# The second residual projection of an encoder layer walked by token tile instead of by column half, and the preparation of the two FFN products moved around it

## The reference, cut to what matters

```python
    om = jnp.einsum('bhqm,bmhd->bqhd', p, mem_v.astype(jnp.float32)).reshape(bx, t, MEM_WIDTH)
    x = x + om.astype(x.dtype) @ w_mo                      # 512 -> 1024 columns
    h = rmsnorm(x, norm_ffn)
    x = x + jnp.square(jax.nn.relu(h @ w_ffn1)) @ w_ffn2   # 1024 -> 4096 -> 1024
```

## Time and profile before

| | |
|---|---|
| runs | 1749.38, 1750.48, 1750.35 us |
| profiled execution | 1747.89 us, its span 1745.9 us, granted clock 0.99 |
| TensorE matmul busy | 1666.5 us, 95% of the span |
| DVE, ACT, POOL busy | 1178.3, 805.7, 33.8 us |
| projection mo | about 938 to 996 us of the span |
| first FFN product | 995 to 1374 us |
| second FFN product | from 1374.8 us |

### The profile page before, as it was taken

How to read it: one execution, slowest core, us unless ns; L and a number is a source line. 1 busy time by engine, 2 the same in 40 slices (tenths; PEclk the granted TensorE clock), 3 DMA queues, 4 the chain that set the end, 5 groups by cost and what they waited for, 6 DMA issues and landing times. The chain is left out here.

```text
span 1745.9 us, 26833 instructions
## 1 busy us (share of the span) xinstructions
PE 1666.5 (95%) x10590; PEld 1483.1 (85%) x10590; DVE 1178.3 (67%) x1742; ACT 805.7 (46%) x1275; POOL 33.8 (2%) x49
## 2 busy tenths in 40 slices
PE   9999999999999988999999979999999999999998
PEld 8877777889999988888977879999999878787876
DVE  6577877666757599557163785656666867767676
ACT  5577777763434356214173543333323333333344
POOL 1000000000000002001000100000000000000001
PEclk9999999999999999999999999999999999999999
DMA  5232121201011242620280313333334933434322
GB/s 191 76 85 78 49 78 49 78 25 51 27 54 39 59 152 87 251 68 25 73 217 14 133 34 131 139 139 139 139 139 168 351 133 129 149 133 157 121 96 110
DMA packets 157694, 190.50 MB, mean 109 GB/s; under 512 B 5505, under 2 KB 117761, under 8 KB 155522
## 3 DMA queue, kind: packets, MB, share of 16 engines
q1 hardware_dynamic: 157570, 188.79, 32.8%
HBM read 134.58 MB, written 54.20 MB: 108 GB/s over the span
## 5 line engine op out<-in xcount | busy, mean ns | idle before, releaser
L620 PE MATMUL PS<-sbuf_h_hi,sbuf_w_hi 128*128 128x384 f32 x600 | 211.7, 353 | 6.0 <-ACT sbuf_g_N L631 2.7
L622 PE MATMUL PS<-sbuf_h_hi,sbuf_w_lo 128*128 128x384 f32 x600 | 201.7, 336 | 0.0
L621 PE MATMUL PS<-sbuf_h_lo,sbuf_w_hi 128*128 128x384 f32 x600 | 201.5, 336 | 0.0
L2656 PE MATMUL PS<-sbuf_ops_w,sbuf_go_u 128*128 128x512 f32 x448 | 177.1, 395 | 8.6 <-DVE sbuf_gg_X L2746 8.6
L2657 PE MATMUL PS<-sbuf_ops_w,sbuf_go_u 128*128 128x512 f32 x448 | 175.5, 392 | 0.0
L2658 PE MATMUL PS<-sbuf_ops_w,sbuf_go_u 128*128 128x512 f32 x448 | 175.4, 391 | 0.0
L2493 PE MATMUL PS<-sbuf_ops_S,sbuf_ops_w 128*128 128x288 f32 x512 | 152.8, 298 | 11.2 <-ACT sbuf_ff_u L2522 4.6
L2497 PE MATMUL PS<-sbuf_ops_S,sbuf_ops_w 128*128 128x288 f32 x512 | 152.5, 298 | 0.0
L2495 PE MATMUL PS<-sbuf_ops_S,sbuf_ops_w 128*128 128x288 f32 x512 | 152.2, 297 | 0.0
L620 PEld LDWEIGHTS PS<-sbuf_h_hi,sbuf_w_hi 128*128 128x128 f32 x600 | 113.2, 189 | 16.2 <-issue 10.0
L2522 ACT ACTIVATE sbuf_ff_u<-PS 128x576 f32<-128x576 f32 x64 | 41.6, 650 | 177.7 <-DMA uD<-sbuf_ff_sums 97.6
(11 more groups left out here) (317 smaller groups left out, 3919.1 us busy)
## 6 DMA issues: line engine op xcount, KB each, us to landing
sbuf_gg_u<-uD SPq DMA_DIRECT2D x28, 1024.0 KB, 5.1
uD<-sbuf_ff_u SPq DMA_DIRECT2D x16, 1152.0 KB, 4.2
sbuf_ff_raw<-w_ffn SPq DMA_DIRECT2D x16, 1024.0 KB, 6.3
sbuf_gg_B<-w_ffn SPq DMA_DIRECT2D x16, 1024.0 KB, 7.8
sbuf_raw<-w_in SPq DMA_DIRECT2D x28, 512.0 KB, 4.8
uD<-sbuf_ff_sums SPq DMA_DIRECT2D x16, 768.0 KB, 6.3
sbuf_X<-x_prompt SPq DMA_DIRECT2D x16, 512.0 KB, 7.3
xD<-sbuf_X SPq DMA_DIRECT2D x9, 512.0 KB, 2.6
```

What stands on the lines that cost most here:

```text
L620: pe.matmul(out, hi, h_hi[:, kb, tok], start=kb == 0, stop=False)
L621: pe.matmul(out, hi, h_lo[:, kb, tok], start=False, stop=False)
L622: last = pe.matmul(out, lo, h_hi[:, kb, tok], start=False, stop=kb == KB - 1)
L2656: pe.matmul(out, u_hi, x_hi, start=first, stop=False, skip_group_check=True)
```

## The change

The projection's two halves are taken in turn: two tiles of half 0 ahead, then (half 1, tile t) and (half 0, tile t + 2) alternating, by the list `MO_SEQ`. So each tile is complete earlier and its norm starts earlier. ACT's and DVE's lists around it (`mo_act`, `mo_dve`) are new. The sums S1 and S2 are cut in two pieces at token 320 of 576 (`CUT`), and S2's raw form shares S4's rows. At the start of the first FFN product the sums, cuts of weights and evacuations stand in another order. In the second product, `add(k, t)` stands ahead of `blocks` instead of behind, and the sums of the last unit come behind the additions of product k = 1. SP loads `u_unit(1)` ahead of the blocks B12 and B22, and stores the last unit after `u_unit(3)`; the load of weight unit 1 comes behind the projection's tile 6.

```diff
-                    *((row_at(a_rows[x][1]), x, (KH, HT)) for x in ("S1", "S2", "S3", "S4")),
+                    *((row_at(a_rows[x][1]), x, (KH, HT)) for x in ("S1", "S3", "S4")),
+        a_raw["S2"] = a_raw["S4"]
...
+        CUT = 5 * HT // 9
+        MO_SEQ = [(0, 0), (0, 1)] + [x for t in range(NT - 2) for x in ((1, t), (0, t + 2))] + [(1, NT - 2), (1, SMP)]
...
+        def mo_act(act):
+            for t in range(NT):
+                norm_square(act, n_ff, t)
+                if 1 <= t < SMP:
+                    ff_high(act, t - 1)
+                if t == SMP - 2:
+                    w_high(act, 0)
+                    w_high(act, 1)
+            act.wait_ge(N["lo"], 2 * (n_ff.base + SMP - 1))
+            sum_high(act, "S1", 0)
+            w_high(act, 2)
+            ff_high(act, SMP - 1)
+            act.wait_ge(a_sum.sem, a_sum.n(1))
+            sum_high(act, "S2", 0)
+            w_high(act, 3)
...
+            added(0, 0)
+            added(0, 1)
+            f_blocks(dve, 0)
+            for t in range(SMP):
+                added(1, t)
+                if t == SMP - 1:
+                    w_low(dve, 0)
+                norm_mean(dve, n_ff, t)
+                if t == SMP - 1:
+                    w_low(dve, 1)
+                norm_scale(dve, n_ff, t)
+                if 1 <= t < SMP - 1:
+                    ff_low(dve, t - 1)
+                if t + 2 < NT:
+                    added(0, t + 2)
+            added(1, SMP)
+            ff_low(dve, SMP - 2)
+            norm_mean(dve, n_ff, SMP)
+            dve.wait_ge(N["lo"], 2 * (n_ff.base + SMP - 1))
+            sum_raw(dve, "S2", "S1", "A11", 0)
+            norm_scale(dve, n_ff, SMP)
+            sum_low(dve, "S1", 0)
+            w_low(dve, 2)
+            ff_low(dve, SMP - 1)
...
+            left_over(FF_AT["P6", 0])
+            act.wait_ge(a_sum.sem, a_sum.n(3))
+            sum_high(act, "S4")
+            left_over(FF_AT["P7", 0])
+            for k in range(9, 13):
+                w_high(act, k)
...
+            out_of("X11", 0)
+            w_low(dve, 3)
+            ff_low(dve, SMP)
+            dve.wait_ge(N["lo"], 2 * (n_ff.base + NT))
+            sum_raw(dve, "S2", "S1", "A11", 1)
+            w_low(dve, 4)
+            sum_low(dve, "S1", 1)
+            w_low(dve, 5)
+            dve.wait_ge(a_sum.sem, a_sum.n(2))
+            sum_low(dve, "S2", 0)
+            sum_low(dve, "S2", 1)
+            w_low(dve, 6)
+            sum_low(dve, "S3")
+            w_low(dve, 7)
+            dve.wait_ge(a_low.sem, a_low.n(4))
+            sum_raw(dve, "S4", "A12", "S2")
+            w_low(dve, 8)
+            out_of("X11", 1)
+            sum_low(dve, "S4")
+            out_of("X22", 0)
+            f_blocks(dve, 1)
+            for k in range(9, 13):
+                w_low(dve, k)
...
                 if by_tile(k) and kb == 0:
                     for t in tiles_of_product(k):
+                        add(k, t)
                         if t in (0, 1):
                             for h in range(2):
                                 blocks(g, ("T4", "T1")[t], h)
-                        add(k, t)
+                    if k == 1:
+                        token_sums(dve, LASTU)
...
             block_unit("B21", 0)
-            block_unit("B12", 0)
-            sp.wait_ge(f_p, FF_AT["P5", LASTU] + 1)
-            block_unit("B22", 0)
             sp.wait_ge(f_p, FF_AT["P7", LASTU] + 1)
             u_unit(1)
+            block_unit("B12", 0)
+            block_unit("B22", 0)
             u_unit(2)
```

More of the change, by code:

```diff
@@ L1767, in out_pe, with out_act @@
                         norm_turn(pe, norm, t - 2)
-        def out_act(act, round0, nkb, norm, first=lambda act, p: None,
-                    between=lambda t: None, after=None):
+        def out_act(act, round0, nkb, norm, first=lambda act, p: None, between=lambda t: None):
             passes = nkb // 2
@@ L2435, in mo_behind, with part, sum_high, sum_low @@
[L2435 to L2439, removed]
+        def part(x, i):
+            return x[:, :, (0, CUT)[i]:(CUT, HT)[i]]
+        def sum_high(act, x, i=None):
+            hi, raw_ = (a_hi[x], a_raw[x]) if i is None else (part(a_hi[x], i), part(a_raw[x], i))
+            act.activation(hi, raw_, ACT.Copy).then_inc(a_cut.sem, 1)
+        def sum_low(dve, x, i=None):
+            dve.wait_ge(a_cut.sem, a_cut.n(SUM_CUT[x, i]))
+            lo, raw_, hi = (y if i is None else part(y, i) for y in (a_lo[x], a_raw[x], a_hi[x].bitcast(F32)))
+            dve.tensor_tensor(lo, raw_, hi, ALU.subtract).then_inc(a_low.sem, 1)
@@ new lines, in sum_raw, with mo_pe @@
+        def sum_raw(dve, x, y, z, i=None):
+            out, p, m = (a_raw[w] if i is None else part(a_raw[w], i) for w in (x, y, z))
+            dve.tensor_tensor(out, p, m, ALU.subtract).then_inc(a_sum.sem, 1)
+        def mo_pe(pe):
+            y, add = mo_s
+            for n, (p, t) in enumerate(MO_SEQ):
+                if t == 0:
+                    for s in pass_slots(p):
+                        wait_unit(pe, unit(R_MO, s), s)
+                if n >= len(MO):
+                    pe.wait_ge(add, n - len(MO) + 1)
+                mo_ready(pe, p, t)
+                out = PS[:, MO[n % len(MO)], :]
+                tok = slice(t * P, (t + 1) * P)
+                for j in range(4):
+                    s = pass_slots(p)[j // 2]
+                    cols = slice((j % 2) * 512, (j % 2 + 1) * 512)
+                    pe.matmul(out, h_hi[:, j, tok], w_hi[s][:, cols], start=j == 0, stop=False)
+                    pe.matmul(out, h_lo[:, j, tok], w_hi[s][:, cols], start=False, stop=False)
+                    last = pe.matmul(out, h_hi[:, j, tok], w_lo[s][:, cols], start=False, stop=j == 3)
+                    if t == SMP and j % 2:
+                        last.then_inc(slot_free[s], 1)
+                if t < SMP:
+                    last.then_inc(y, 1)
+                if p and 1 <= t < SMP:
+                    if t == 2:
+                        pe.wait_ge(CN["lo"], len(ogroups))
+                    norm_turn(pe, n_ff, t - 1)
@@ L2506, in ff1_act, with left_over @@
         def ff1_act(act):
[L2507 to L2512, removed]
+            def left_over(s):
+                what, n = FF[s]
                 if what in ("P1", "P6", "P7", "P4"):
@@ L2564, in out_of @@
                 dve.wait_ge(x_sq.sem, x_sq.n(n + 1))
[L2565 to L2576, removed]
+                if n < LASTU:
+                    token_sums(dve, n)
@@ L3107, in _ @@
             load_gain(a["norm_ffn"], D)
-            for s in range(2):
-                sp.wait_ge(slot_free[s], unit(R_MO, s)[0] + 2)
-            pair_unit(1)
             for t in range(NT):
-                sp.wait_ge(mo_s[1], NT + t + 1)
+                if t == SMP - 1:
+                    for s in range(2):
+                        sp.wait_ge(slot_free[s], unit(R_MO, s)[0] + 2)
+                    pair_unit(1)
+                sp.wait_ge(mo_s[1], MO_AT[1, t] + 1)
                 sp.dma_start(xD[t], X[:, t, :]).then_inc(xl[t], 16)
```

112 lines of the change are left out of this document (56 added, 56 removed).

## The result

The changed kernel takes 1738.71 us (median of 4 runs, 1738.27 to 1741.96) beside 1750.23 for the kernel before (4 runs): the ratio is 0.9941, 95% interval 0.9929 to 0.9953. That is 11.5 us less, where 19.5 were forecast; 1738.71 lies just above the range. The profiled execution is the slowest of the four, 1741.96 us.

What follows compares the result with a forecast made beforehand. TensorE, busy for 95% of the span, was taken as the bound, so only its waits and clock could be won. 11.6 + 7.0 + 0.9 = 19.5 us off 1750.35 gave 1730.8 us, range 1727 to 1738.5.

Steps and rivals of the forecast that it cites:

- The projection, 0: Projection: same matmuls, additions and transposes in another order; no gain taken for it.
- Start of the first product, 11.6 us: Start of the first FFN product: shorter TensorE waits give 11.6 us, two half-clock stretches of 1.6 and 1.7 included.
- The steps up to P4: First product's start: P1 of unit 1 at 1004.0, P5 1011.0, P6 1014.15, P7 1018.35, P4 1022.95.
- From here on all runs as before: First product, past P6 of unit 1: nothing further changes, so the 11.6 us gained are kept.
- C: Rival, chance 0.14: loads come late, of weight unit 1 (3 us) or in the second product (2 to 5); 1733 to 1740.
- Start of the second product, 7.0 us: Second product before T3's addition: 4.2 us less waiting and 2.8 for the clock, with 0.3 of 4.5 left.
- the other turns, 0.9: Second product at k = 8, 15, 22: the same order takes away 0.43 each; two seen, 0.9 us counted.
- its alternative: Second product's start: loads share evenly, `u_unit(1)` lands at 1381.6 as before; gain 2.3 us, or 5.1 with the clock.
- The sums moved behind k = 1 cost 2.7 there ... covered, by 1 us: Second product: TensorE's two ready pieces last 5.5 us, DVE needs 4.5 to the third, so the moved sums cost nothing.
- the row of the prediction: DVE's 2304-column instructions: 2.55 us long but 2.47 from start to start, so most of the fixed cost is hidden.
- the rule weighed beside it: Cutting S1 and S2: each DVE instruction pays a fixed cost; three more cost about 0.5 us, 19.1 instead of 19.6.
- Rival B: Chance 0.20: clock falls before P1 of unit 1, around P4 (1.6 each) or at k = 1 (up to 2.8); 1732 to 1737.

Runs made afterwards that it cites:

- first_only: The kernel before with the projection's and the first product's edits alone, the second product's undone: 1740.67 us, ratio 0.9959.
- evac_first: The changed kernel with DVE's low cuts of weight pieces 17 and 18 in unit 1 behind the evacuation of P5: 1737.68 us, ratio 0.9931.
- second_only: The kernel before with the second product's edits alone (addition first, last unit's sums behind k = 1, loads ahead of the store): 1746.52 us, ratio 0.9987.
- sums_back: The changed kernel with the last unit's sums and its store back at their old places: 1734.97 us, ratio 0.9916.
- store_later: The changed kernel with only the last unit's store one place later, behind u_unit(4): 1738.77 us, ratio 0.9933.
- evac_first_k2: The changed kernel with evac_first's order, the last unit's sums behind the additions of k = 2 and its store ahead of u_unit(6): 1730.43 us, ratio 0.9890.
- whole_sums: The changed kernel with S1 and S2 summed and cut whole again, behind the last tile: 1741.09 us, ratio 0.9948.
- after_again: The changed kernel measured once more, unaltered, as a base on the same chip: 1740.98 us, ratio 0.9948.
- pool_blocks: The changed kernel with last unit's sums and store later, a weight cut ahead of unit 2's block sums, unit 1's block sums on POOL: 1734.19 us, ratio 0.9907.

## Why the forecast was off

**The projection, 0**: right. The only wait left there is one of 0.2 us for `sbuf_xn`.

**Start of the first product, 11.6 us.** The steps up to P4 came as listed, with about 1 us less. The profiled execution was 3.2 us late when it came to the projection (its first matmul at 941.17, in the kernel before at 937.95), in stages that the edit doesn't touch; less that, P4 began at 1024.2 where 1023 was forecast, 10.7 us ahead of the kernel before. The waits were 2.34, 0.74 and 0.74 where 1.8, 1.0 and 1.4 were forecast, and the three others under 0.3. What failed is the sentence "From here on all runs as before". In the two traces as they stand TensorE had been moved 7.5 us ahead at that point, and the load of the third weight pair by 4.75, since DVE's list of sums had only been reordered and not shortened. If the starts of TensorE's matmuls are compared one by one, counted from the same one of the cross attention, the lead of 10.7 us holds up to P3 of unit 1 and is 6.4 behind it: the displaced wait and the lower clock behind it cost 4.3. first_only puts the part at 7.2 us in place of 11.6, and evac_first gives 3.3 back by removing that one wait. Of the rivals this is C's kind (a load comes late), at a load that C didn't name; the one that it named, of weight unit 1, was issued at 991.30, and ACT cut it at 1002.08 without a wait.

**Start of the second product, 7.0 us, and the other turns, 0.9.** The wait at k = 1 went as forecast, to 0.62 (0.3 was written), and the clock stayed up: counted in the same way from the second product's first matmul, the changed kernel gained 6.7 us there of the 7.0. The loads also queued as the prediction read from its row and not as its alternative had it. ACT had `u_unit(1)` 8.6 us after its issue at 1364.11, in place of 13.7, and T3 began 6.9 us after the product's first matmul (1371.28), where 6.8 was forecast. ACT's and DVE's timelines in the changed kernel:

```profile
1372.73 1.16 ACT L2344 ACTIVATE sbuf_go_u<-sbuf_gg_u 128x512 fp32r<-128x512 f32 x2 [0.56 <-DMA sbuf_gg_u<-uD]
```

```profile
1378.21 2.36 DVE L2853 TENSOR_TENSOR sbuf_gg_T<-sbuf_gg_B 128x1024 f32<-128x1024 f32 x2 [1.56 <-issue]
```

What failed is "The sums moved behind k = 1 cost 2.7 there ... covered, by 1 us". I counted what TensorE had ready, and not what else was behind the sums in DVE's list: the cut that releases `u_unit(4)`. That load takes 7.3 us to ACT, so 2.7 us of sums there came back as 4.52 one product later, and the clock's loss with them, 7.0 us in all by the same count. second_only puts the part at 2.3 us in place of 7.9. The shares of sums (nearly all) and store (0.9 us) come from sums_back and store_later.

The term of 0.9 us for the other turns was too small: they gave 2.7, 0.9 in each of three. The prediction saw two of the waits of 0.43 us, and there are three. TensorE's timeline in the kernel before has these besides the one at 1490.35:

```profile
1579.18 0.50 PE L2656 MATMUL PS<-sbuf_ops_w,sbuf_go_u 128*128 128x512 f32 x1 [0.43 <-DVE sbuf_gg_X L2746]
...
1667.98 0.50 PE L2656 MATMUL PS<-sbuf_ops_w,sbuf_go_u 128*128 128x512 f32 x1 [0.43 <-DVE sbuf_gg_X L2746]
```

Each also costs more than its idle time: the matmul at it starts 0.82 us after the one ahead of it, in the changed kernel 0.23.

**The sum.** With both displaced waits removed and the rest of the change in place, the kernel takes 1730.43 us, and 1730.8 was the forecast. That the two agree so closely is luck, as a split of the profiles shows. From a matmul of the cross attention that waits 0.4 us for ACT in each of them (881.22 in the kernel before, 884.45 in the changed one, 883.49 in evac_first_k2) to the first matmul of the second product (1374.82, 1371.28, 1367.62) it is 493.6, 486.8 and 484.1 us; from there to the last matmul (1738.28, 1732.37, 1721.51) it is 363.5, 361.1 and 353.9. So the first product gives 9.5 of the 11.6 in this profile, and the second 9.6 where 7.9 were forecast: 6.9 at its start and 2.7 in the other turns. Two wrong terms offset each other. In the changed kernel the same split gives 6.8 and 2.4, together 9.1, and with the 3.2 us of late start taken off that is the 5.9 us between its profiled execution and that of the kernel before.

Two slips of the prediction's working changed little. One sentence starts from a sum of 19.6, where the sum is 19.5. And ACT's cut of 2304 columns was put at 2.05 us by DVE's slope, which gives 2.5; it took 2.13.

**The halves of S1 and S2.** The trace agrees with the row of the prediction and not with the rule weighed beside it. S2's two low pieces took 2.53 us from start to start and S3's whole one 2.46, both in the changed kernel:

```profile
1015.35 2.62 DVE L2430 TENSOR_TENSOR sbuf_ops_S<-sbuf_ff_S,sbuf_ops_S 128x1280 fp32r<-128x1280 f32 x2
1017.88 0.68 DVE L2323 TENSOR_TENSOR sbuf_ops_w<-sbuf_ff_T,sbuf_ops_w 128x512 fp32r<-128x512 f32 x1
1018.49 2.55 DVE L2430 TENSOR_TENSOR sbuf_ops_S<-sbuf_ff_S,sbuf_ops_S 128x2304 fp32r<-128x2304 f32 x1
1020.95 0.68 DVE L2323 TENSOR_TENSOR sbuf_ops_w<-sbuf_ff_T,sbuf_ops_w 128x512 fp32r<-128x512 f32 x1
```

The difference is 0.07, where 0.08 was estimated. By the Trainium skill, VectorE: DVE Perf Modes, on the TRN2 errata, it would be 0.16, an estimate from its fixed part of 151 in (N + 151) / 0.96 ns. The halves also bring nothing that can be measured: whole_sums is as fast as after_again.

**The clock.** Rival B was given 0.20 for a fall before P1 of unit 1 or elsewhere. In the profile of the changed kernel it fell there (0.65 over 4 us), and so in six of eleven profiles, see below; by the profiles 0.20 was low. What it adds to the medians isn't shown.

Still open: what the rest of the wait before P1 of unit 1 is, 2.34 in place of 1.8 (DVE waits 0.50 for POOL ahead of the last scaling, at 1002.89, which the list left out and which may be most of it), and how much of the 3 us between executions of one kernel lies in earlier stages.

## What to carry to other kernels

When a change moves the bounding engine ahead by some microseconds, list what does not move with it: every store, load and evacuation that is released by another engine's list. Follow each to its next use, past the end of the edit. Work that is moved to where the bounding engine is covered must also be asked what stands behind it in its own engine's list, and whether one of those releases a transfer. A transfer of some 7 us turns a short delay into a longer one a stage later. And where a wait is for an instruction whose inputs are ready, look first at what is ahead of it in its list, not at how to make the late thing earlier: of the 2.4 us of wait the kernels that moved the load's issue or the work ahead of it left 1.5 to 2.2, and one change of order left none.

## What the hardware showed

After the same wait before P1 of unit 1, 2.3 to 2.4 us long, the granted clock from 1004 to 1030 us was 0.93 in six profiles and 1.00 in five. The code up to that wait is the same in all eleven. The Trainium skill, TensorE: Matmul & The Clock Gate, says that the look at activity runs free of the program; by that rule this is what one expects, and the trace agrees. The longest waits of the second product, of 4.5 us, were followed by the lower clock in all seven profiles that had one, but at a different price. In first_only 13 matmuls behind the wait start 0.43 us apart, where 0.23 is the pace at full clock, 2.8 us lost; in second_only and evac_first there are 7, 1.5 us.

DVE was slower while POOL ran tensor_tensor on SBUF beside it (pool_blocks): its cut of 2304 columns took 3.63 us in place of 2.55. POOL's four instructions of 128x512 took 1.28 to 3.58, the longest beside that cut; no run shows POOL's alone.

A load of 1 MB behind a store of 1.9 MB on SP's queue reached ACT 9.1 to 9.8 us after the store's last issue in all 14 profiles, whether it was issued 3.1 or 0.5 us behind it.
